# Four index products inside each of four projection units, in place of two behind each of eight

## What is computed

```
x = layer_norm(x, emb_ln_g, emb_ln_b)
u_pool, q, c, iq, ik, iw = split(x @ w_in)      # 512, 512, 128, 512, 64, 8 columns
pooled = trailing-window means of u_pool (windows 2, 4, 8, 16) minus the token, then one 128x128 map per group
score[t, s] = sum_h iw[t, h] * relu(iq[t, h] . ik[s] / 8)        # the indexer, 8 heads
idx = causal top-k of score (k = 256)
attention over the selected latents with relative bias, softmax, 8 heads
x = layer_norm(ALPHA * x + concat(pool, attention) @ w_o)
x = layer_norm(ALPHA * x + relu(x @ w_up)**2 @ w_down)
```

## Time and profile before

| | |
|---|---|
| median of three runs | 1264.47 us (1264.08 to 1264.97) |
| the profiled execution | 1263.58 us |
| its span (first to last instruction) | 1261.8 us |
| PE busy | 1208.7 us, 96% |
| DVE busy | 833.4 us, 66% |
| ACT busy | 557.7 us, 44% |
| POOL busy | 512.5 us, 41% |
| mean granted clock of PE | 0.992 of full speed |

### The profile page before, as it was taken

One profiled execution on the slowest core, in us unless ns is written; L12 is line 12 of the kernel. 1 busy time (PEld: TensorE's weight loads), 2 busy tenths in 40 slices (PEclk: granted clock), 3 DMA queues, 4 the chain that ended last, 5 costly groups with the idle time before them and its releaser, 6 DMA issues.

```text
span 1261.8 us, 16530 instructions
## 1 busy us (share of the span) xinstructions
PE 1208.7 (96%) x5761; PEld 979.6 (78%) x5761; DVE 833.4 (66%) x1201; ACT 557.7 (44%) x943; POOL 512.5 (41%) x370
## 2 busy tenths in 40 slices
PE   5999997989999999999999999989899999999997
PEld 3776785778788778788788789978788888888886
DVE  6388989557857888888988766647534233243357
ACT  4546542775165234244243366652342442433440
POOL 2235798424435676775865752202102102103002
PEclk9999999899999999999999999999999999999999
DMA  7723431101314333243242200024132333423331
GB/s 221 250 76 106 145 100 52 66 1 34 101 34 134 100 101 117 84 133 100 84 132 90 94 1 2 1 101 134 63 100 88 105 101 95 117 84 99 116 102 66
DMA packets 126564, 117.59 MB, mean 93 GB/s; under 512 B 5741, under 2 KB 99498, under 8 KB 126506
## 3 DMA queue, kind: packets, MB, share of 16 engines
q1 hardware_dynamic: 126506, 116.81, 30.4%
HBM read 106.29 MB, written 10.50 MB: 93 GB/s over the span
## 4 chain that ended last, share of the span: by engine, by line
PE 84%; DVE 6%; POOL 5%; ACT 2%; issue 2%; DMA 1%; POOLq 0%; DVEq 0%; ACTq 0%
PE g_bank L1540 16%; PE g_bank L1542 16%; PE g_bank L1541 16%; PE wide L1540 9%; PE wide L1542 9%; PE wide L1541 9%; PE g_bank L1500 4%; POOL wlo L417 2%; PE wide L1645 1%; DVE win L588 1%; PE wide L1604 1%; PE wide L1605 1%; PE g_bank L1692 1%; POOL rows L805 1%; POOL rstd L745 1%
## 5 line engine op out<-in xcount | busy, mean ns | idle before, releaser
L417 POOL TENSOR_TENSOR wlo<-wring,whi 128x1024 fp32r<-128x1024 f32 (+1 forms) x94 | 229.6, 2444 | 226.0 <-ACT whi L1413 121.7
L1540 PE MATMUL g_bank<-xhi,whi 128*128 128x512 f32 (+2 forms) x768 | 300.7, 392 | 4.8 <-DVE xlo L654 3.8
L1542 PE MATMUL g_bank<-xhi,wlo 128*128 128x512 f32 (+2 forms) x768 | 296.9, 387 | 0.0
L1541 PE MATMUL g_bank<-xlo,whi 128*128 128x512 f32 (+2 forms) x768 | 296.8, 386 | 0.0
L1413 ACT ACTIVATE whi<-wring 128x1024 fp32r<-128x1024 f32 x120 | 127.1, 1059 | 355.8 <-PE wide L1542 179.8
L417 DVE TENSOR_TENSOR wlo<-wring,whi 128x1024 fp32r<-128x1024 f32 (+1 forms) x66 | 84.4, 1279 | 197.6 <-ACT whi L1413 192.7
L1540 PE MATMUL wide<-whi,hhi 128*128 128x512 f32 x480 | 190.2, 396 | 0.7 <-POOL wlo L417 0.7
L1542 PE MATMUL wide<-whi,hlo 128*128 128x512 f32 x480 | 189.6, 395 | 0.0
L1541 PE MATMUL wide<-wlo,hhi 128*128 128x512 f32 x480 | 189.6, 395 | 0.0
L1540 PEld LDWEIGHTS g_bank<-xhi,whi 128*128 128x128 f32 (+1 forms) x768 | 143.8, 187 | 39.9 <-DVE xlo L654 4.3
L1541 PEld LDWEIGHTS g_bank<-xlo,whi 128*128 128x128 f32 (+1 forms) x768 | 143.9, 187 | 33.0 <-issue 1.8
(11 more groups left out here) (215 smaller groups left out, 1993.4 us busy)
## 6 DMA issues: line engine op xcount, KB each, us to landing
wring<-in_w_up SPq DMA_DIRECT2D x64, 512.0 KB, 4.0
wring<-in_w_down SPq DMA_DIRECT2D x64, 512.0 KB, 3.7
wring<-in_w_in SPq DMA_DIRECT2D x26, 512.0 KB, 3.9
wring<-in_w_o SPq DMA_DIRECT2D x16, 512.0 KB, 4.6
rows<-in_x SPq DMA_DIRECT2D x8, 512.0 KB, 5.0
normalized_rows<-rows SPq DMA_DIRECT2D x8, 512.0 KB, 6.9
rows<-normalized_rows SPq DMA_DIRECT2D x4, 512.0 KB, 5.2
emb_stage<-normalized_rows SPq DMA_DIRECT2D x4, 512.0 KB, 4.8
```

The source lines that it names most:

```text
L417: eng.tensor_tensor(parts_of(name, lo_tile(name)), parts_of(name, wring[n % 4]), parts_of(name, hi_tile(name)).bitcast(F32), ALU.subtract) ...
L1540: nc.tensor.matmul(out_ap, w_hi, m_hi, start=first, stop=False)
L1541: nc.tensor.matmul(out_ap, w_hi, m_lo, start=False, stop=False)
L1542: return nc.tensor.matmul(out_ap, w_lo, m_hi, start=False, stop=last)
```

## The change

`unit_dots` gives units 1 to 4 (u1, u2, u3, q0) of chunk 0 four index products each. PE issues them inside the unit, one ahead of each of the last four steps over the depth; `column_products` could already take such products in the MLP, where there are six, and now counts from the end. ACT rectifies a unit's four products ahead of that unit's rounding and copy. DVE adds four, then does one pooling, four times; all five steps of `normalize` follow, then selection. In POOL's list the inverse deviations go in pairs: of row blocks 0 and 1 ahead of q2's split, of 2 and 3 ahead of q3's.

```diff
+        def unit_dots(c, unit):
+
+            return range(4 * unit - 4, 4 * unit) if c == 0 and 1 <= unit <= 4 else ()
...
-            inverse_std(EMB1, [0])
+            inverse_std(EMB1, [0, 1])
             lo(("q", 0, 2))
-            inverse_std(EMB1, [1])
+            inverse_std(EMB1, [2, 3])
             lo(("q", 0, 3))
-            inverse_std(EMB1, [2, 3])
             diagonals((2, 3))
...
-            for n in range(8):
-                if n < 4:
-                    next(pooled)
-                add_score(2 * n)
-                add_score(2 * n + 1)
-                if n >= 3:
-
-                    next(normalized)
+            for unit in range(1, 5):
+                for d in unit_dots(0, unit):
+                    add_score(d)
+                next(pooled)
+            for b in normalized:
+                pass
             select_pair()
...
+                    for d in unit_dots(c, unit):
+                        relu_dots(d)
                     hi_after(name)
...
-                    if c == 0:
-                        relu_dots(2 * unit)
-                        relu_dots(2 * unit + 1)
                     unit += 1
...
                 for k in range(KT):
-                    if dots and k >= 2:
-                        dot(dots[k - 2])
+                    if k >= KT - len(dots):
+                        dot(dots[k - KT])
...
-                    project(name)
-                    if c == 0:
-                        dot(2 * unit)
-                        dot(2 * unit + 1)
+                    project(name, None, unit_dots(c, unit))
                     unit += 1
```

More of the change, by code:

```diff
@@ L1554, in column_products, with project @@
                 return ins
-            def project(name, x_parts=None):
+            def project(name, x_parts=None, dots=()):
                 pe.wait_ge(*LO[name])
@@ L1559, in project @@
                 m = KEYW if name[0] == "ik" else P
-                column_products(bank(name)[0:m, :], R[name] % 2, x_parts).then_inc(g_full, 1)
+                column_products(bank(name)[0:m, :], R[name] % 2, x_parts, dots).then_inc(g_full, 1)
             def keys_queries(c):
```

## The result

The changed kernel takes 1274.77 us (median of 4 runs, 1273.43 to 1276.12), the kernel before it beside it 1264.28 us (1263.96 to 1264.97): a ratio of 1.0072, 95% interval 1.0059 to 1.0084. It is 10.5 us slower; 8.0 were forecast. Its profiled execution took 1275.79 us, its span 1274.0, 12.2 more than that of before.

The account below looks back on a forecast made before the run. PE, working nearly all the time, was taken as the bound; 6.35 us of shift to `near` plus 1.6 of slow clock made 8.0, so 1264.47 + 8.0 = 1272.4 us, range 1267.5 to 1276.

Parts of the forecast that it names:

- Index products on PE: Units u1 to q0 in chunk 0: the same 32 matmuls, no PE product waits for ACT; cost 0.
- DVE to statistics 1: Chunk 0, DVE from sum 3 at 71.5 us: 26.1 us of work plus 6.6 of stalls, ending at 104.2 us.
- the stalls: Three POOL weight splits in chunk 0 each hold up a DVE pooling by 2.2 us, 6.6 in all.
- rival a: Chunk 0: a split misses DVE; one missed and no clock fall gives 1268.6 us, two 1267; chance 0.18.
- The new wait: Ahead of q2, PE stands 6.3 us for a split queued behind statistics 0 and 1; `near` 6.35 us later.
- The clock: At q2's start PE's granted clock is on its lower level after the long hole, costing 1.6 us.
- the slow first matmul: Between q2's start and `near`: a first matmul of 0.61 against 0.23 us, counted as gone.
- Sum to `near`: Chunk 0 up to `near`: 6.35 us of shift plus 1.6 of slow clock, 8.0 us later.
- Selection, chunk 1: Selection starts near 115.3 us, 1.6 earlier, ends near 187.5; DVE then idles, gaining 0 for chunk 1's pooling.
- rival (c): Faster: chunk 1's poolings escape POOL's splits, up to 11.1 us gained against 8.0 lost, 1261.4 us; chance 0.04.
- repeats 8 us later: After selection, the stretch up to attention was to recur unchanged, only 8 us later.

Follow-up runs that it names:

- experiment 2: Changed kernel with POOL's splits of q2's and q3's weights ahead of all four inverse deviations: 1272.52 us, ratio 1.0056 to the kernel before.
- experiment 4: Changed kernel with 24 idle-work transposes on PE ahead of q2's product: 1273.87 us, ratio 1.0074 to the kernel before.
- experiment 1: The changed kernel run and profiled again with no edit: 1274.53 us, ratio 1.0069 to the kernel before.
- experiment 10: Kernel before with POOL's eight gains behind the last attention mask and chunk 1's splits in four pieces: 1269.61 us, ratio 1.0028.
- experiment 3: Kernel before with only the change's POOL order, inverse deviations in pairs ahead of q2's and q3's splits: 1279.91 us, ratio 1.0120.
- experiment 6: Changed kernel with POOL's splits of chunk 0's u and q weights in four pieces of 256 columns: 1276.57 us, ratio 1.0080 to the kernel before.
- experiment 9: Kernel before with POOL's eight gain instructions moved behind the last attention mask: 1268.77 us, ratio 1.0027.
- experiment 5: Changed kernel with the first two row blocks' statistics ahead of pooling 3 on DVE: 1275.32 us, ratio 1.0080 to the kernel before.
- experiment 12: Kernel before with three gains left in place, five in twenty pieces behind attention masks 12 to 31: 1257.85 us, ratio 0.9949.

## Why the prediction was right, point by point

Times of the first profile are given less its 1.66 us.

- **Index products on PE: 0.** Held. No unit waits.
- **DVE to statistics 1.** Sum 3 ended at 71.5, as said, and statistics 1 at 104.0 against 104.2. The parts were a little off both ways: the stalls came to 2.1, 1.9 and 1.9, 6.0 in place of 6.6, and sums of block 3 waited 0.75 us for ACT, which the sum had at nothing. That the total fits is in part luck. No split missed DVE (rival a), and that they hold it up by most of their length is seen again in experiment 2, where two more of them cost pooling 3 its 4.2 us.
- **The new wait.** PE was through with po3 at 102.4 where the sum had 101.9, and q2 began at 107.8 where it had 108.2. So the profile gives PE 5.43 us of idle time where 6.3 were worked out. q2's start moved by 8.2 us in both profiles, counted from u0.
- **The clock.** The fall was foreseen, and the slow time lasted 4.6 us from the restart, where 3.0 to 5.8 had been the bounds. The stretch from q2's start to `near` took 13.4 us where 11.15 + 1.6 = 12.75 were counted. Experiment 4 has it at the upper level: 11.5 us. So the clock cost 1.9 to 2.0 in place of 1.6, and the other 0.3 is that the sum took the slow first matmul away whole: in experiment 4 the first matmuls of q2 and q3 still take 0.34 us from start to start, not 0.23, and the last of q2 takes 0.30.
- **Sum to `near`.** 8.0 forecast; 8.2 and 8.3 in two profiles, counted from u0. q2 came 0.4 earlier than summed and the stretch behind it took 0.6 more, so it is closer than its terms.
- **Selection, chunk 1.** It started at 114.5 (115.3 forecast, 116.93 before) and ended at 181.3, where 187.5 was forecast: it took 66.8 us in place of 72.1, since its copies and sums at both ends met less of POOL's work (its first instruction takes 0.36 us where it took 1.56). It gained nothing, as was said: DVE then idled 17.8 us and the 7.1 us hole repeated, so rival (c) failed on its own first condition: the first pooling waited for ACT's copy with the split beside it.
- **The forecast's gap.** The median moved by 10.5 us, 2.5 more than the sum (in experiment 1's group by 8.5, half a microsecond more). What the sum put at nothing is the stretch behind `near`, with the sentence that it "repeats 8 us later". This did not hold in full: the slow clock at chunk 1's first product lasts longer and costs 1.3 us in both profiles. From `near` to the first pooling of chunk 1 are 76.6 us before and 77.9 in the changed kernel both times. Of the five profiles with before's chunk 0, four have 76.4 to 76.7 and experiment 10 has 77.1. Of the nine others, seven have 77.5 to 78.0, experiment 3 has 77.1 and experiment 6 has 76.1. It is not the fall at q2 that does it: experiment 4, with a clock of 1.00 there, has 77.5. What decides how long the clock stays low there stays open. The rest of the gap in the profiles is the slow stretch behind 340 us, which is not of the change.
- **What was not seen.** The hole of chunk 1 was read as made by the stalls beside POOL's instructions, and experiment 9 shows it: of ten such instructions five are gains, and without these the hole is 0.69 us. But the prediction counted it only as something that would repeat. The five gains had no need to stand there.

## What to carry to other kernels

Before an engine's work is reordered, list what is queued behind each wait on the engines that feed it: here the weight that the matrix engine wanted stood behind a few tiny instructions that waited for statistics. Where two engines shut each other out, moving one wait only moves the bill (experiments 2 and 5); what pays is to move the work that nobody is waiting for to where the other engine works on operands that don't meet it, and in small pieces. Eight long instructions in a row undid the whole gain (experiment 9); with three of them left in place and the other five in twenty pieces it was kept (experiment 12).

## What the runs showed of the hardware

DVE gets its turn between POOL's instructions even where these follow back to back: pieces of 256 columns make several stalls of about 0.5 us where one instruction of 1024 made one of 2 us (experiment 6), and all stalls of chunk 0's poolings together shrank only from 6.0 to 5.3 us, so cutting helps only where few of DVE's instructions meet the pieces. In experiment 9 four of them stood beside long ones in a row and took 9.92 us in place of 2.50.

What DVE does decides whether it is held up. Beside POOL's work the row statistics (`stats<-rows`, 0.65 to 0.70 each in all fourteen profiles) and attention's logits and probabilities, which read `wide` or `g_bank` (0.69 and 0.69 with and without a piece beside them), keep their time; copies, the poolings' sums and the row normalization (2.23 against 0.76) don't. The Trainium skill ("SBUF — State Buffer", section "Who interferes with whom") says that VectorE contends with GpSimd when it has two SBUF inputs (with a GpSimd instruction that reads SBUF) or runs a copy or tensor-scalar form in a two-port mode, and not with a single SBUF input outside these; all of the rows above agree.

The clock's length of stay is not a constant of the program. After PE went on, the lower level lasted 3.0 us at chunk 1's first product before the change and 6.0 behind it, 4.6 at q2, and the same light stretch at the start of attention (PE idle 0.69 and 1.53 us between small products) fell to 0.50 from 218 us on in the profile of experiment 9 and stayed at 1.00 in that of 12. Differences of a microsecond or two between single profiles of these kernels can be that alone.
